# A kernel's prologue reordered: weight loads asked for at once, one round trip on another queue, copies and a share of a product on other engines

## The reference, cut to what matters

```python
c_act = jax.nn.silu(c)
for l in range(DEPTH):
    mod = c_act @ w_ada[l] + b_ada[l]                  # (1, 1024) @ (1024, 6144)
    sh1, sc1, g1, sh2, sc2, g2 = jnp.split(mod, N_MOD, axis=-1)
    h = modulate(rms_norm(x, mixer_norm_g[l]), sh1, sc1)
    proj = h @ w_in[l]
    ...
```

## Time and profile before

| | us |
|---|---|
| median of 3 runs | 2534.82 (2534.06 to 2535.74) |
| the profiled execution | 2535.56 |
| its span, first to last instruction | 2533.8 |
| PE / DVE / ACT busy | 2236.6 / 1639.0 / 1017.6 |

### The profile page before, as it was taken

One profiled execution on the slowest core, in us unless ns is written; L12 is line 12 of the kernel. 1 busy time (PEld: TensorE's weight loads), 2 busy tenths in 40 slices (PEclk: granted clock), 3 DMA queues, 4 the chain that ended last, 5 costly groups with the idle time before them and its releaser, 6 DMA issues.

```text
span 2533.8 us, 33157 instructions
## 1 busy us (share of the span) xinstructions
PE 2236.6 (88%) x12627; PEld 1945.0 (77%) x12627; DVE 1639.0 (65%) x2311; ACT 1017.6 (40%) x1484; POOL 58.3 (2%) x111
## 2 busy tenths in 40 slices
PE   4998899975999799985799899789969998988997
PEld 3887688864788588874699876679969996667997
DVE  5785799976685798985588605374547872346553
ACT  1121578743121477752433403244433342223343
POOL 0100000000100000000000000000000000000000
PEclk7998899997998899997899995899989999778998
DMA  8657298864648198866489631466537993013830
GB/s 275 212 174 282 117 414 350 344 257 167 220 158 310 73 421 344 342 256 257 158 311 324 209 117 50 161 212 209 167 106 251 331 315 100 17 42 115 276 116 17
DMA packets 252027, 543.44 MB, mean 214 GB/s; under 512 B 14290, under 2 KB 172524, under 8 KB 227308
## 3 DMA queue, kind: packets, MB, share of 16 engines
q1 hardware_dynamic: 251852, 541.50, 58.9%
q10 hardware_dynamic: 32, 0.02, 0.0%
HBM read 540.42 MB, written 1.07 MB: 214 GB/s over the span
## 4 chain that ended last, share of the span: by engine, by line
PE 78%; DVE 13%; issue 3%; DMA 3%; ACT 2%; SPq 1%; DVEq 0%; POOL 0%; ACTq 0%; POOLq 0%
PE ps L586 19%; PE ps L619 9%; PE ps L621 9%; PE ps L620 9%; PE ps L680 4%; DVE acc L1461 4%; PE ps L682 4%; PE ps L681 4%; PE ps L598 4%; DVE ring_lo L1732 2%; PE ps L720 2%; PE ps L722 2%; PE ps L721 2%; PE ps L606 2%; DVE std L1484 1%
## 5 line engine op out<-in xcount | busy, mean ns | idle before, releaser
L1732 DVE TENSOR_TENSOR ring_lo<-ring,wsg 128x1024 fp32r<-128x1024 f32 x384 | 458.9, 1223 | 87.4 <-ACT wsg L1223 83.8
L586 PE MATMUL ps<-arena,ring 128*128 128x256 f32 (+1 forms) x2016 | 441.6, 386 | 23.4 <-DVE arena L1973 15.5
L1501 DVE TENSOR_TENSOR wsp<-ring,wsp 128x1024 fp32r<-128x1024 f32 x264 | 321.5, 1223 | 213.6 <-ACT wsp L1179 206.5
L1223 ACT ACTIVATE wsg<-ring 128x1024 fp32r<-128x1024 f32 x384 | 404.4, 1059 | 128.6 <-PE ps L682 65.8
L586 PEld LDWEIGHTS ps<-arena,ring 128*128 128x128 f32 (+1 forms) x2016 | 371.4, 187 | 89.3 <-DVE arena L1973 16.3
L619 PE MATMUL ps<-hsp,wsp 128*128 128x256 f32 x1408 | 406.4, 289 | 35.6 <-DVE hsp L1522 18.6
L1179 ACT ACTIVATE wsp<-ring 128x1024 fp32r<-128x1024 f32 x264 | 277.2, 1055 | 365.9 <-PE ps L621 322.8
L620 PE MATMUL ps<-hsp,wsp 128*128 128x256 f32 x1408 | 403.0, 286 | 0.0
L621 PE MATMUL ps<-hsp,wsp 128*128 128x256 f32 x1408 | 402.9, 286 | 0.0
L619 PEld LDWEIGHTS ps<-hsp,wsp 128*128 128x128 f32 x1408 | 275.0, 195 | 39.0 <-DVE wsp L1501 23.5
L680 PE MATMUL ps<-wsg,hsg 128*128 128x512 f32 x512 | 218.3, 426 | 68.1 <-DVE ring_lo L1732 68.1
(11 more groups left out here) (216 smaller groups left out, 2778.4 us busy)
## 6 DMA issues: line engine op xcount, KB each, us to landing
ring<-in_w_expert_gate_dram SPq DMA_DIRECT2D x64, 1024.0 KB, 7.9
ring<-in_w_expert_up_dram SPq DMA_DIRECT2D x64, 1024.0 KB, 9.9
ring<-in_w_expert_down_dram SPq DMA_DIRECT2D x64, 1024.0 KB, 5.9
ring<-in_ada_w_dram SPq DMA_DIRECT2D x48, 1152.0 KB, 8.4
ring<-in_ffn_w_gate_dram SPq DMA_DIRECT2D x44, 1024.0 KB, 11.1
ring<-in_ffn_w_up_dram SPq DMA_DIRECT2D x44, 1024.0 KB, 13.6
ring<-in_ffn_w_down_dram SPq DMA_DIRECT2D x44, 1024.0 KB, 5.2
ring<-in_w_ada_dram SPq DMA_DIRECT2D x32, 1152.0 KB, 9.4
```

Of the source, the lines that this page charges most:

```text
L586: last = mm(dst, wk(k), rhs(k), start=(k == 0), stop=(k == n - 1))
L1223: act_(high_piece(n % HIGHS, j), piece(EXPERT_1[e], j), ACT.Identity).then_inc(S.whi, 1)
L1501: v_.tensor_tensor(split_part(at % SPLITS, 1, n), piece(unit, n), split_part(at % SPLITS, 0, n, F32), ALU.subtract).then_inc(S.wlo, 1)
L1732: v_.tensor_tensor(low_piece(EXPERT_1[e], j), piece(EXPERT_1[e], j), high_piece(n % HIGHS, j, F32), ALU.subtract).then_inc(S.wlo, 1)
```

## The change

SP asks for modulation units 0, 1 and 2 in a row, with nothing between them; `rows_1` comes behind the nine DMAs. The Toeplitz load moves from SP's queue to ACT's, right behind the write that it depends on. ACT, and no longer DVE, copies the transposed x and the 8 bias results out of PSUM. PE's first wait counts `init_v` to 3 and `bias_w` to 1, where it counted `init_v` to 4. DVE multiplies units 0 and 1 as before, and of unit 2 only row groups 0 to 3. Row groups 4 to 7 of unit 2 are multiplied on PE: 24 matmul calls (4 row groups by 6 columns of 128) with the weights as the stationary operand and one column of `cvec` as the moving one, into the same six PSUM columns into which PE then sums DVE's half. PE, and no longer DVE, releases unit 2's slot.

```diff
+FIRST_DVE = 4
@@ SP
             for u in range(AHEAD):
                 acquire(0, 0, u)
                 ada_columns(u, a.w_ada, 0, slice(u * COLS, (u + 1) * COLS))
-                if u == 0:
-                    sp.wait_ge(init_t, 1)
-                    rows_1(0)
-                    sp.wait_ge(bias_r, 16)
-                    toeplitz = bass.AP(scratch.tensor, 0, [[1, P], [384, NH], [1, T]])
-                    sp.dma_start(ring[:, 3, 0:NH * T].rearrange("p (h t) -> p h t", h=NH), toeplitz
-                                 ).then_inc(bias_r, 16)
+            sp.wait_ge(init_t, 1)
+            rows_1(0)
@@ PE
-            pe.wait_ge(init_v, 4)
+            pe.wait_ge(init_v, 3)
+            pe.wait_ge(bias_w, 1)
             pe.wait_ge(bias_r, 32)
...
-            for u in range(AHEAD):
+            for u in range(AHEAD - 1):
                 ada_sum(u, u % 2, 0, u * AC)
+            u = AHEAD - 1
+            wait_landed(pe, 0, 0, u)
+            for k in range(FIRST_DVE, KD):
+                for c in range(AC):
+                    mm(ps[:, 0, u * AC + c:u * AC + c + 1], wada(u)[:, k, c * P:(c + 1) * P], cvec[:, k:k + 1],
+                       start=(k == FIRST_DVE and c == 0), stop=False, skip_group_check=True)
+            pe.wait_ge(S.ada_acc, u + 1)
+            for c in range(AC):
+                last = mm(ps[:, 0, u * AC + c:u * AC + c + 1], acc[:, u % 2, c * P:(c + 1) * P], ones[:, 0:1],
+                          start=False, stop=True, skip_group_check=True)
+            last.then_inc(S.ada_sum, 1)
+            pe.wait_ge(S.ada_sum, u + 1)
+            release(pe, u)
@@ ACT, behind the write of the bias rows to scratch
+            eng.wait_ge(bias_r, 16)
+            toeplitz = bass.AP(scratch.tensor, 0, [[1, P], [384, NH], [1, T]])
+            eng.dma_start(ring[:, 3, 0:NH * T].rearrange("p (h t) -> p h t", h=NH), toeplitz).then_inc(bias_r, 16)
+            eng.wait_ge(init_t, 3)
+            xf = x[:].rearrange("p k t -> p (k t)")
+            for j in range(4):
+                last = act_(xf[:, j * 512:(j + 1) * 512], ps[:, j, :], ACT.Identity)
+            last.then_inc(init_v, 1)
+            for i in range(NH // 2):
+                eng.wait_ge(init_t, 4 + i)
+                act_(bias[:, 2 * i:2 * i + 2, :], ps[:, 4 + i % 4, :].rearrange("p (c t) -> p c t", c=2), ACT.Identity
+                     ).then_inc(bias_m, 1)
@@ DVE
-            ...
+            for u in range(AHEAD - 1):
+                ada_unit(0, 0, u, u, u % 2, cvec)
+            u = AHEAD - 1
+            wait_landed(eng, 0, 0, u)
+            eng.wait_ge(S.ada_sum, u - 1)
+            (row groups 0 to FIRST_DVE - 1 of unit 2, as in ada_unit)
             keep_ahead(AHEAD, 0)
```

More of the change, by code:

```diff
@@ L1537, in _ @@
                              gb.rearrange("p k t -> p (k t)")[0:NH, 0:384], ALU.add).then_inc(bias_w, 1)
-            eng.wait_ge(init_t, 3)
-            xf = x[:].rearrange("p k t -> p (k t)")
             eng.wait_ge(init_v, 2)
[L1541 to L1551, removed]
-                ada_unit(0, 0, u, u, u % 2, cvec)
+            for u in range(AHEAD - 1):
+                ada_unit(0, 0, u, u, u % 2, cvec)
+            u = AHEAD - 1
+            wait_landed(eng, 0, 0, u)
+            eng.wait_ge(S.ada_sum, u - 1)
+            v_.tensor_scalar(acc[:, u % 2, :], wada(u)[:, 0, :], cvec[:, 0:1], None, ALU.mult).then_inc(S.ada_part, 1)
+            for k in range(1, FIRST_DVE):
+                eng.wait_ge(S.ada_part, u * (KD - 1) + k)
+                last = v_.scalar_tensor_tensor(acc[:, u % 2, :], wada(u)[:, k, :], cvec[:, k:k + 1], acc[:, u % 2, :],
+                                               ALU.mult, ALU.add)
+                last.then_inc(S.ada_part if k < FIRST_DVE - 1 else S.ada_acc, 1)
             keep_ahead(AHEAD, 0)
```

## The result

The changed kernel took 2540.77 us (median of 17 runs, 2538.85 to 2550.98), the kernel before beside it 2534.12 (17 runs). The ratio is 1.0030 with a 95% interval of 1.0022 to 1.0037: 5.6 to 9.4 us slower. The profiled execution took 2539.41 with a span of 2537.7, 3.9 us more than the span before. The forecast was slower, 2546.0, with a range of 2534.5 to 2549.

What follows compares the result with a forecast made beforehand. The prologue's chain of waits, ending with PE's last `ada_sum` at 52.82, was taken as the bound. With the Toeplitz load at 38.8 it ends at 64.0, 11.2 us later: 2535.56 becomes 2546.8, less 0.74 is 2546.0; range 2534.5 to 2549.

Steps and rivals of the forecast that it cites:

- The Toeplitz landing: Prologue: the Toeplitz load on ACT's queue lands at 38.8, where it landed at 24.18 before.
- strictly last: Prologue queues: bound in which the Toeplitz load lands only at the end of all transfers, 38.8.
- by rows: Prologue queues: they take turns row by row, so the Toeplitz load lands at 38.8 and unit 1 at 27.5.
- by bytes: Prologue queues: bytes shared half and half, so the Toeplitz load lands at 29.4 and unit 1 at 30.8.
- The two `ada_sum` and the bias products: PE in the prologue: bias products 39.0 to 47.7, then `ada_sum` 0 and 1, warm, 1.47 each, to 51.2.
- The 48: PE's one-column instructions for half of unit 2: 8 at full clock to 52.2, 40 at 0.227 to 61.3.
- The sum: Prologue's end with Toeplitz at 38.8: PE's last `ada_sum` ends at 64.0 against 52.82, 11.2 us later.
- late case: Toeplitz load lands at 38.8; time 2546.0, own range 2543 to 2549; chance 0.60.
- early case: Rival: Toeplitz load lands between 24.2 and 29.4, prologue ends 1.5 to 2.4 us later, time 2536.8; chance 0.33.
- Full clock in the stream: Rival: PE's 48 take 5.9 us, not 10.9, with an early Toeplitz load; time 2529.7 or 2532.2; chance 0.07.
- The copies, costed at nothing: Prologue: x and bias copies moved from DVE to ACT, 0.597 each for the x copies; effect nil.

Runs made afterwards that it cites:

- experiment with short rows: Changed kernel with units 1 and 2 asked for in rows of 1024 B in place of 3072 B; ratio 1.0009 (1.0001 to 1.0018).
- experiment with the load on SP's queue: Changed kernel with the Toeplitz load and row loads back on SP's queue between units 0 and 1; ratio 0.9998 (0.9989 to 1.0007).
- second comparison: Changed kernel, unaltered, run once more against the kernel before on the same chip; ratio 1.0038 (1.0024 to 1.0052).
- third unit back on DVE: Changed kernel with unit 2 multiplied wholly on DVE again, Toeplitz load still on ACT's queue; ratio 1.0016 (1.0007 to 1.0025).
- copies alone: Kernel before with only the copies moved from DVE to ACT; ratio 0.9980 (0.9971 to 0.9989).
- wide matmuls between: Changed kernel with one unused 512-column matmul call behind each of the four row groups that PE multiplies; ratio 1.0049 (1.0036 to 1.0063).
- load behind unit 1: Changed kernel with Toeplitz load on SP's queue behind unit 1, unit 0's `ada_sum` ahead of the bias products, unit 2 on DVE; ratio 0.9978, median 2526.92.
- the same, a quarter on PE: The kernel with the load behind unit 1, but row groups 6 and 7 of unit 2 multiplied on PE; ratio 0.9974, median 2527.59.
- 12 useless instructions: Kernel before with 12 tiny useless copies added to ACT's list in the prologue; ratio 0.9982 (0.9974 to 0.9991).

## Why the prediction was right, point by point

**The Toeplitz landing.** Predicted 38.8, measured 38.79. That number by itself proves little: it follows from the volume as soon as the load is not favoured, and strictly last would have given it too. That the queues share by rows and not by bytes is shown by the rows of each queue, 95 against 95 from 26 to 27 above, and by the experiment with short rows, in which the share of the bytes went from a quarter to a half. Unit 1 fits: it landed at 26.55 (predicted 27.5 by rows, 30.8 by bytes; strictly first it would have been there by 25). One term was mis-sized and cost nothing: the load was to start 1.5 us after its issue, and started after 3.6. Stretches of the changed kernel, columns as in the earlier trace rows:

```profile
17.00:18.00 1.00, 0.00 (x0) 0.00 (x0) 0.96 (x2) 1.00 (x3) 0.00 (x0) 1.00 1.04 421
...
20.00:21.00 1.00, 0.00 (x0) 0.00 (x0) 0.96 (x2) 0.00 (x0) 0.00 (x0) 1.00 1.05 388
...
36.00:37.00 1.00, 0.00 (x0) 0.00 (x0) 0.00 (x0) 0.00 (x0) 0.00 (x0) 1.00 1.07 356
```

The long rows alone, then both kinds mixed, then mostly short rows. The link never idles before 37 (in each us from 15 on its DMA share is 1.03 or more), so the end of all the volume stays where it was predicted. The Trainium skill, page "DMA: Bandwidth & Descriptors", section "Queues, rings and completion order", has turns of several descriptors each; with equal counts the shares are the same, and these runs agree with that but can't tell one from the other.

**The two `ada_sum` and the bias products.** Predicted done at 51.2, measured 51.35, by two errors that cancel. The bias products took 9.33 us where 8.7 were taken, and the two sums with their gap ended 3.1 us behind them where 3.5 were taken. How late in the bias products the clock rises is chance (8.67 to 10.06 us for them in the profiles of this study). The PEclk column reads 1.00 there all along in this profile, but their first instructions take 1193 ns and the later ones 592: durations have to be read beside it.

**The 48.** The mechanism was right (they begin warm and turn cold), the size was 2 us too large: 10.1 us predicted, 8.06 measured. Two terms. The clock fell at 53.6, 5.4 us after the bias products ended, where I had taken 4 to 4.9 from the rows; so some 20 instructions ran warm, not 8. That too varies: in the second profile it fell 4.7 us after them, and the 48 took 8.68. And a cold one costs 213 ns (from 42.49 to 52.73 for 48 in the experiment with the load on SP's queue), not 227: I had divided a group's whole duration by 12, with the tail of its last instruction in it. The same tail makes the last sum 2.57, not 2.72. The mean of the 48 was 168 ns, where 227 was named as the sign. Stretches of the changed kernel:

```profile
52.00:53.00 1.00, 1.00 (x12) 1.00 (x11) 0.96 (x2) 0.00 (x0) 0.00 (x0) 1.00 1.11 370
53.00:54.00 1.00, 1.00 (x10) 1.00 (x9) 0.94 (x1) 0.00 (x0) 0.00 (x0) 0.81 1.08 350
54.00:55.00 1.00, 1.00 (x6) 1.00 (x6) 0.00 (x0) 0.00 (x0) 0.00 (x0) 0.50 1.09 351
```

Twelve instructions in the first microsecond, six in the last. The Trainium skill's rule that TensorE gets its full clock by being kept busy (page "TensorE: Matmul & The Clock Gate", section "Why this matters for your kernels") does not hold for such a stream: by their records PE and PEld were busy all the time, and the clock fell.

**The sum.** Predicted +11.2 at the prologue's end, measured +9.16, and 2.0 of the difference are the terms above. Against the second profile of the kernel before the shift is 8.2. The changed kernel's time rose by 5.6 to 9.4 us, and by 6.1 to 13.2 in the second comparison: 8.2 and 9.2 are in both. So the time, 2540.77, lies in the stated range, but 5.2 us under the forecast and under the late case's own range (2543 to 2549). The stated range holds it only because it was made wide for the early case, which did not happen; so far it is luck. Of the 5.2, 0.7 is the median that the forecast started from (2534.82, against 2534.12 beside the changed kernel), and 2.0 are the terms above; the other 2.5 are open, and less than two profiles of one kernel differ by.

**What was missed.** ACT's list grew by 12 instructions (1484 to 1496), and no time was put on that. ACT's wait at the second layer's start is 3.98 and 4.08 us in the two profiles of before, 3.15 and 3.37 in those of the changed kernel. Every kernel with the copies on ACT can be held against its prologue (us from the kernel before; the prologue by its first and by its second profile):

| | prologue's end moved | time moved |
|---|---|---|
| changed | +9.2, +8.2 | +5.6 to +9.4 |
| load back on SP's queue | +2.6, +1.7 | -2.8 to +1.8 |
| third unit back on DVE | +8.0, +7.1 | +1.8 to +6.3 |
| copies alone | -1.8, -2.7 | -7.3 to -2.8 |
| shorter rows | +3.2, +2.3 | +0.3 to +4.6 |
| wide matmuls between | +16.1, +15.1 | +9.1 to +16.0 |
| load behind unit 1 | -3.1, -4.1 | -8.1 to -3.3 |
| the same, a quarter on PE | -3.3, -4.2 | -8.9 to -4.1 |
| 12 useless instructions | +0.7, -0.2 | -6.6 to -2.3 |

By the first profile of before most gain more than their prologue explains; by the second only the third unit on DVE and, just, the copies alone do. Only the 12 useless instructions stand far out by both, and a profile shows 1 us of that. Where the rest comes from is open: it is not in any one row, and the profiles of one kernel differ among themselves by more.

**The rivals.** The early load is out: 38.8. Had it come true its price would have been about right: with the load at 24, the half on PE ended 2.6 us later than before, against +2.4 predicted. Full clock in the stream is out. The copies, costed at nothing, are what moves the prologue's end forward when they stand alone, by 1.8 to 2.7 us. How much of the 2.8 to 7.3 us in the time is theirs is not shown, since 12 useless instructions in ACT's list gave 2.3 to 6.6 without any copy.

**Best version.** The load behind unit 1 on SP's queue, copies on ACT, unit 2 on DVE: 2526.92 us, 6.1 us below the kernel before beside it (2532.98), 3.3 to 8.1 by its interval. It beats both kernels; 3.1 to 4.1 of it is in the prologue. From the copies alone (0.9971 to 0.9989) and from the version with a quarter on PE these runs do not tell it apart.

## What to carry to other kernels

In this kernel a load that others waited for did not get faster on a queue of its own while another queue was full: it took 23.1 us in place of 8.3. The two queues moved as many rows as each other, so the load with 1024 B rows beside one with 3072 B rows got a quarter of the bytes, and half when the rows were alike. Put such a load in the one queue at the place where it is needed, and ask what the engine that waits for it has queued behind. Before a share of a vector engine's work goes to TensorE in matmuls one column wide, price it at the slower clock as well: here 48 instructions took 8.1 to 10.2 us, where DVE's four operations took 4.2. Measure each part of a change alone. And take more than one profile of the kernel before: two of them differed by 1.0 us in the prologue, a ninth of the effect to be explained.

## What the runs showed of the hardware that was not expected

The first rows of a transfer on an idle queue beside a full one moved 3.6 to 4.0 us after its issue (19.2 for an issue at 15.65, 19.7 for one at 15.72), where on a drained link it took 1.5. One matmul call of 512 columns behind every 12 one-column instructions (each call 2.05 us long) left the granted clock at 0.50. And twelve instructions without any effect, in an engine that was idle, went with a time 0.18% shorter (0.09 to 0.26% by the intervals of several runs each); the part of it that a profile shows is that the engine waited 1 us less at the head of its loop.
